# Three rounded products for each unrounded one in the causal and the cross attention of the last layer

## What is computed

```python
h = rms_norm(x, norm_g)
(qa, ka, va, ga, ub, vb, gb, qc, gc, ma, mb, mc) = split_cols(h @ w_in, IN_SPLITS)
qa, ka = partial_rope(qa, pos), partial_rope(ka, pos)          # 6 heads of 128
out_a = moba_attention(qa, ka, va) * silu(ga)                  # causal softmax(q k^T / sqrt(128)) v
out_b = gmlp_spatial_gate(ub, vb, ...) * silu(gb)
mk, mv = split(rms_norm(mem, mem_norm_g) @ w_mem_kv, 2)
out_c = softmax(qc @ mk^T / sqrt(128)) @ mv * silu(gc)         # 4 heads of 128
y = sigmoid(ma) * (out_a @ w_branch_a) + sigmoid(mb) * (out_b @ w_branch_b) + sigmoid(mc) * (out_c @ w_branch_c)
x = x + y @ w_out
```

## Time and profile before

| what | value |
|---|---|
| median of 3 runs | 913.99 us (913.52 to 914.01) |
| the profiled execution | 914.61 us |
| its span from first to last instruction | 912.4 us |
| granted TensorE clock | 1.000 |
| TensorE busy | 99% of the span |
| its weight loads busy | 84% |
| VectorE, ScalarE, GpSimd busy | 67%, 56%, 4% |
| DMA | 169.32 MB, mean 186 GB/s |

### The profile page before, as it was taken

The page is one execution under the profiler, slowest core; times in us unless marked ns, Lnnn a source line. Parts: engine busy times, 40 slices in busy tenths (PEclk is TensorE's granted clock), DMA queues, the critical chain, the costliest instruction groups (busy, mean ns, idle before and its releaser), DMA issues.

```text
span 912.4 us, 12831 instructions
## 1 busy us (share of the span) xinstructions
PE 904.5 (99%) x4764; PEld 764.8 (84%) x4764; DVE 610.7 (67%) x1007; ACT 507.8 (56%) x820; POOL 40.4 (4%) x53
## 2 busy tenths in 40 slices
PE   9999999999999999999999999999999999999997
PEld 7888788888888898878888888887888888888886
DVE  4897697766663756769766666386656577574665
ACT  5786655555562456665555555255557664655444
POOL 0100000440000001000000000001000000000000
PEclk9999999999999999999999999999999999999999
DMA  9844526777573577552855556354664465555651
GB/s 322 294 164 139 185 93 231 233 228 249 192 238 112 108 225 231 159 187 93 293 183 190 198 190 241 122 171 149 198 201 131 159 202 166 167 157 186 198 169 72
DMA packets 72604, 169.32 MB, mean 186 GB/s; under 512 B 11288, under 2 KB 32944, under 8 KB 71904
## 3 DMA queue, kind: packets, MB, share of 16 engines
q1 hardware_dynamic: 70080, 157.73, 53.3%
q0 software_dynamic: 2320, 10.58, 3.5%
q10 hardware_dynamic: 144, 0.20, 0.1%
HBM read 167.43 MB, written 1.06 MB: 185 GB/s over the span
## 4 chain that ended last, share of the span: by engine, by line
PE 95%; DVE 2%; DMA 1%; ACT 1%; SPq 0%; issue 0%; DVEq 0%; ACTq 0%
PE psum L851 20%; PE psum L1037 14%; PE psum L732 8%; PE psum L737 8%; PE psum L734 8%; PE psum L1040 8%; PE psum L1069 7%; PE psum L1073 4%; PE psum L962 3%; PE psum L972 3%; PE psum L966 3%; PE psum L1173 2%; PE psum L709 1%; PE psum L1208 1%; PE psum L1189 1%; DMA stage<-in_w_ab_in 1%
## 5 line engine op out<-in xcount | busy, mean ns | idle before, releaser
L1792 DVE TENSOR_TENSOR base_lo<-stage,base_hi 128x1024 fp32r<-128x1024 f32 (+3 forms) x221 | 261.1, 1206 | 103.9 <-ACT base_hi L1373 102.7
L1373 ACT CAST base_hi<-stage 128x1024 fp32r<-128x1024 f32 (+3 forms) x221 | 222.5, 1035 | 57.2 <-PE psum L737 22.5
L1792 DVE TENSOR_TENSOR extra_lo<-stage,extra_hi 128x1024 fp32r<-128x1024 f32 (+1 forms) x68 | 80.7, 1212 | 45.6 <-ACT extra_hi L1373 45.4
L732 PE MATMUL psum<-base_hi,xt 128*128 128x512 f32 (+2 forms) x256 | 100.7, 393 | 0.0
L737 PE MATMUL psum<-base_hi,xt 128*128 128x512 f32 (+2 forms) x256 | 98.4, 384 | 0.0
L734 PE MATMUL psum<-base_lo,xt 128*128 128x512 f32 (+2 forms) x256 | 98.2, 384 | 0.0
L1373 ACT CAST extra_hi<-stage 128x1024 fp32r<-128x1024 f32 (+1 forms) x68 | 68.1, 1029 | 46.8 <-PE psum L851 35.5
L851 PE MATMUL psum<-base_hi,ht 128*128 128x512 f32 x288 | 87.5, 393 | 0.3 <-DVE qk_t L2249 0.3
L1037 PE MATMUL psum<-xt,extra_hi 128*128 128x512 f32 x320 | 80.0, 392 | 0.0
L1037 PEld LDWEIGHTS psum<-xt,extra_hi 128*128 128x128 f32 x320 | 58.2, 189 | 10.8
L851 PEld LDWEIGHTS psum<-base_hi,ht 128*128 128x128 f32 x288 | 53.7, 188 | 12.5 <-DVE qk_t L2249 0.7
(11 more groups left out here) (265 smaller groups left out, 1538.9 us busy)
## 6 DMA issues: line engine op xcount, KB each, us to landing
stage<-in_w_up SPq DMA_DIRECT2D x80, 512.0 KB, 4.6
stage<-in_w_down SPq DMA_DIRECT2D x44, 512.0 KB, 4.4
stage<-in_w_in_a SPq DMA_DIRECT2D x22, 512.0 KB, 4.7
stage<-in_w_cd_in SPq DMA_DIRECT2D x16, 512.0 KB, 4.8
stage<-in_w_in_b SPq DMA_DIRECT2D x12, 512.0 KB, 3.6
stage<-in_w_ab_in SPq DMA_DIRECT2D x12, 480.0 KB, 6.8
ln_par<-in_ln POOLq DMA_DIRECT2D x4, 1024.0 KB, 7.6
stage<-in_w_ab_out SPq DMA_DIRECT2D x8, 512.0 KB, 3.7
```

Source lines behind the costliest of these rows:

```text
L732: pe.matmul(acc, ah, wh, start=(k == 0), stop=False)
L1373: act.copy(w_hi(c, 0, w), stage_of(c, w)).then_inc(hi_done, 1)
L1792: dve.tensor_tensor(w_lo(c, 0, w), stage_of(c, w), w_hi(c, 0, w).bitcast(F32), ALU.subtract).then_inc(lo_done, 1)
```

## The change

Every product of the ten heads becomes three of rounded operands, `hi*hi + hi*lo + lo*hi`, as in the gemms. The copies of ScalarE that already stand there write the high parts (their target gets the rounded type); VectorE makes the low parts as the difference of the source in PSUM and the high part. New are:

- `qk_low`, in VectorE's slot s, for head s: 512 columns, between the maximum and the due base_lo (causal only). TensorE's logits wait for it (`qk_lows`), and so do the transposes of the next head.
- `probs_low`, at the end of VectorE's slot s, for head s-2: 384 columns (causal) or 512 (cross). PV and the transposes of the next head's probabilities wait for it (`p_lows`).
- the high part of the causal values, 1536 columns, by ScalarE behind its slot 1, and the low part by VectorE behind its slot 2; PV waits for it (`moba_v_los`).
- the high and low parts of the cross keys, values and queries, 1024 columns each, by ScalarE at the chunks 3, 4, 5 of `gate_a` and by VectorE at 4, 5, 6; the first cross logits wait for all three (`cross_los`).

The parts lie in memory that is free by then (the hidden activations' buffer, the arena), some in the place of their source. No transfer is added.

```diff
...
@@ TensorE, slot @@
                 if stream == "moba" and h < hi_h:
                     if h >= 1:
                         pe.wait_ge(qk_copied, h)
+                        pe.wait_ge(qk_lows, h)
...
                     if h >= 1:
                         pe.wait_ge(head_done, h)
+                    pe.wait_ge(p_lows, h + 1)
+                    if stream == "moba":
+                        pe.wait_ge(moba_v_los, 1)
+                        v_hi, v_lo, p_lo, at = moba_v_hi, moba_v_lo, moba_p_lo, h * HD2
+                    else:
+                        v_hi, v_lo, p_lo, at = cross_v_hi, cross_v_lo, cross_p_lo, (h - MOBA_H) * HD2
                     for kt in range(TT):
                         first = 0 if hd.full else kt * P
-                        last = pe.matmul(psum[:, O_BANK, first:S], hd.v(kt),
-                                         probs_t[:, h % 2, kt * S:kt * S + S - first], start=(kt == 0), stop=(kt == 1))
+                        acc, cut = psum[:, O_BANK, first:S], slice(kt * S, kt * S + S - first)
+                        pe.matmul(acc, v_hi[:, kt, at:at + HD2], cross_p_hi[:, h % 2, cut], start=(kt == 0), stop=False)
+                        pe.matmul(acc, v_hi[:, kt, at:at + HD2], p_lo[:, h % 2, cut], start=False, stop=False)
+                        last = pe.matmul(acc, v_lo[:, kt, at:at + HD2], cross_p_hi[:, h % 2, cut], start=False,
+                                         stop=(kt == 1))
...
                         pe.wait_ge(p_copied, h)
+                        pe.wait_ge(p_lows, h)
...
+                    if stream == "xa":
+                        n = h - MOBA_H
+                        pe.wait_ge(cross_los, 3)
+                        for t in range(TT):
+                            acc = psum[:, LOGIT_BANK, t * S:(t + 1) * S]
+                            q_hi, q_lo = [m[:, n, t * P:(t + 1) * P] for m in (cross_q_hi, cross_q_lo)]
+                            pe.matmul(acc, q_hi, cross_k_hi[:, n, :], start=True, stop=False)
+                            pe.matmul(acc, q_hi, cross_k_lo[:, n, :], start=False, stop=False)
+                            last = pe.matmul(acc, q_lo, cross_k_hi[:, n, :], start=False, stop=True)
+                        last.then_inc(logits_ready, 1)
+                        return
+                    pe.wait_ge(qk_copied, h + 1)
+                    pe.wait_ge(qk_lows, h + 1)
+                    hi, lo = moba_qk_hi[:, h % 2, :], moba_qk_lo[:, h % 2, :]
                     for t in range(TT):
                         nk = S if t else n0
-                        last = pe.matmul(psum[:, LOGIT_BANK, t * n0:t * n0 + nk], q[:, t * P:(t + 1) * P], k[:, 0:nk],
-                                         start=True, stop=True)
+                        acc, q, k = psum[:, LOGIT_BANK, t * n0:t * n0 + nk], slice(t * P, (t + 1) * P), slice(S, S + nk)
+                        pe.matmul(acc, hi[:, q], hi[:, k], start=True, stop=False)
+                        pe.matmul(acc, hi[:, q], lo[:, k], start=False, stop=False)
+                        last = pe.matmul(acc, lo[:, q], hi[:, k], start=False, stop=True)
...
@@ ScalarE @@
-                    act.copy(qk_t[:, h % 2, :], psum[:, QK_BANK, :]).then_inc(qk_copied, 1)
+                    act.copy(moba_qk_hi[:, h % 2, :], psum[:, QK_BANK, :]).then_inc(qk_copied, 1)
...
-                    act.copy(probs_t[:, h % 2, 0:w], psum[:, PT_BANK, 0:w]).then_inc(p_copied, 1)
+                    act.copy(cross_p_hi[:, h % 2, 0:w], psum[:, PT_BANK, 0:w]).then_inc(p_copied, 1)
...
+            def moba_v_high():
+                slot("moba", 1)
+                act.copy(moba_v_hi[:, :, :], a2[:, :, 2 * AW:3 * AW]).then_inc(moba_v_his, 1)
...
+                                  3: lambda: cross_hi(cross_k_hi[:, :, :], mem_k, read("mem_k", 2)),
+                                  4: lambda: cross_hi(cross_v_hi[:, :, :], mem_v, read("mem_v", 1)),
+                                  5: lambda: cross_hi(cross_q_hi[:, :, :], q_c, read("in_c", 2)), 7: xa_first})
...
@@ VectorE, slot @@
+                def probs_low():
+                    g = lo_h + s - 2
+                    if lo_h <= g < hi_h:
+                        lows, w = (moba_p_lo, 3 * P) if stream == "moba" else (cross_p_lo, 4 * P)
+                        dve.wait_ge(p_copied, g + 1)
+                        dve.tensor_tensor(lows[:, g % 2, 0:w], psum[:, PT_BANK, 0:w],
+                                          cross_p_hi[:, g % 2, 0:w].bitcast(F32), ALU.subtract).then_inc(p_lows, 1)
+
+                def qk_low():
+                    g = lo_h + s
+                    if stream == "moba" and g < hi_h:
+                        dve.wait_ge(qk_copied, g + 1)
+                        dve.tensor_tensor(moba_qk_lo[:, g % 2, :], psum[:, QK_BANK, :],
+                                          moba_qk_hi[:, g % 2, :].bitcast(F32), ALU.subtract).then_inc(qk_lows, 1)
+
                 h = lo_h + s - 1
                 if not lo_h <= h < hi_h:
+                    qk_low()
+                    probs_low()
                     return
...
+                qk_low()
                 split_to(done["due"])
                 dve.wait_ge(exp_ready, h + 1)
...
                 last.then_inc(head_scaled, 1)
+                probs_low()
...
+            def moba_v_low():
+                slot("moba", 2)
+                dve.wait_ge(moba_v_his, 1)
+                v = a2[:, :, 2 * AW:3 * AW]
+                dve.tensor_tensor(moba_v_lo, v, moba_v_hi[:, :, :].bitcast(F32), ALU.subtract).then_inc(moba_v_los, 1)
...
+                                  4: lambda: cross_low(1, cross_k_lo[:, :, :], mem_k, cross_k_hi[:, :, :]),
+                                  5: lambda: cross_low(2, cross_v_lo[:, :, :], mem_v, cross_v_hi[:, :, :]),
+                                  6: lambda: cross_low(3, cross_q_lo[:, :, :], q_c, cross_q_hi[:, :, :]), 7: slots("xa", 1)})
...
```

More of the change, by code:

```diff
@@ L305, in build_program @@
         arena = sb("arena", [P, ARENA])
+        rounded = lambda name, at, shape: nc.alloc_sbuf_tensor_at(name, [P, *shape], F32R, offset=at)
+        cross_q_hi, cross_k_hi = [rounded(f"cross_{m}_hi", arena_at + 4 * (B2 + n * XA_H * S), [XA_H, S])
+                                  for n, m in enumerate("qk")]
+        cross_v_hi = rounded("cross_v_hi", arena_at + 4 * (B2 + 2 * XA_H * S), [TT, CW])
+        cross_p_lo = rounded("cross_p_lo", arena_at + 4 * (B2 + 3 * XA_H * S), [2, 2 * S])
+        cross_q_lo = rounded("cross_q_lo", arena_at + 4 * A2, [XA_H, S])
+        cross_k_lo = rounded("cross_k_lo", arena_at + 4 * MEM_K, [XA_H, S])
+        cross_v_lo = rounded("cross_v_lo", arena_at + 4 * MEM_V, [TT, CW])
         extra_hi = nc.alloc_sbuf_tensor_at("extra_hi", [P, NS, SLOT], F32R, offset=arena_at + 4 * EXTRA)
@@ L310, in build_program @@
         no_mask = sb("no_mask", [P, 256])
+        qk_t_at = nc.sbuf_base
         qk_t = sb("qk_t", [P, 2, 512])
+        moba_qk_hi = rounded("moba_qk_hi", qk_t_at, [2, 2 * S])
         pair_probs = sb("pair_probs", [P, 4, 384])
@@ L314, in build_program @@
         pair_st = sb("pair_st", [P, 2, 5, 4])
+        probs_t_at = nc.sbuf_base
         probs_t = sb("probs_t", [P, 2, 512])
+        cross_p_hi = rounded("cross_p_hi", probs_t_at, [2, 2 * S])
+        moba_v_lo = rounded("moba_v_lo", arena_at + 4 * A2, [TT, 3 * AW])[:, :, 2 * AW:3 * AW]
+        moba_v_hi = rounded("moba_v_hi", ht_at + 4 * 2 * S * 6, [TT, AW])
+        moba_qk_lo = rounded("moba_qk_lo", ht_at + 4 * 2 * S * 9, [2, 2 * S])
+        moba_p_lo = rounded("moba_p_lo", ht_at + 4 * 2 * S * 11, [2, 2 * S])
         ln_par = sb("ln_par", [P, 2, D])
@@ L362, in build_program @@
         p_turned, p_copied = sem("p_turned"), sem("p_copied")
+        cross_his, cross_los, p_lows = sem("cross_his"), sem("cross_los"), sem("p_lows")
+        qk_lows, moba_v_his, moba_v_los = sem("qk_lows"), sem("moba_v_his"), sem("moba_v_los")
         pv_ready, head_done = sem("pv_ready"), sem("head_done")
@@ L1712, in last_gates @@
                 slot("moba", 0)
-            gemm("in_b", columns_from(2560), {0: last_gates, **{s: slots("moba", s) for s in range(1, 10)},
+            def moba_v_high():
+                slot("moba", 1)
+                act.copy(moba_v_hi[:, :, :], a2[:, :, 2 * AW:3 * AW]).then_inc(moba_v_his, 1)
+            gemm("in_b", columns_from(2560), {0: last_gates, 1: moba_v_high,
+                                              **{s: slots("moba", s) for s in range(2, 10)},
                                               14: lambda: [deviation(4, 0, 1), deviation(4, 1, 1)]})
@@ L2309, in gmlp_norm @@
                 last.then_inc(vn_ready, 1)
-            gemm("in_b", None, {**{s: slots("moba", s) for s in range(1, 10)}, 13: gmlp_stats, 15: gmlp_norm})
+            def moba_v_low():
[3 more added lines that the diff above has]
+                dve.tensor_tensor(moba_v_lo, v, moba_v_hi[:, :, :].bitcast(F32), ALU.subtract).then_inc(moba_v_los, 1)
```

(9 more changed lines are left out.)

10 lines of the change are left out of this document (4 added, 6 removed).

## The result

The changed kernel takes 926.29 us (median of 4 executions, 924.36 to 926.68) against 914.0 before: ratio 1.0132, 95% interval 1.0117 to 1.0147. The forecast was 927.2 us, with 923 to 932 as its range. The profiled execution took 924.36 us, the fastest of the four, with a span of 922.1 us against 912.4.

What follows compares the result with a forecast made beforehand. The prediction took always-busy TensorE to bound the kernel, so its added time and new waits count: -1.9 + 3.4 (products) + 11.7 (waits) = +13.2 us, 927.8 on the profiled execution, 927.2 on the median, range 923 to 932.

Steps and rivals of the forecast that it cites:

- The waits: TensorE in both attentions idles for VectorE's late low parts: 7.5 us causal plus 4.2 cross, 11.7 us in all.
- The 0.2 us from VectorE's end to PV: Estimate added to each wait for the signal and the weight load TensorE can't start ahead: 0.2 us.
- The products: Three rounded products per unrounded one in both attentions: 1.9 us gained at 256 columns, 3.4 us lost at 128.
- the term of the narrow ones: Twelve causal products of 128 columns, each rounded one taken at 0.167 us: 3.4 us of loss, ends 1.8 and 5.1.
- The load row: Weight load on TensorE at 0.83 ns a column, 107 ns for 128 columns, would set the pace of narrow products.
- The clock: Rival: standing still in slot 3 and nine times in all drops TensorE's clock to 1.2 GHz; 930 to 933 us, chance 0.08.
- The main step: TensorE gets new idle time waiting for VectorE's subtractions in both attentions, 11.7 us, which can't be made up later.
- Edits at nothing: ScalarE's high part of V, cross casts and lows in gate_a, later base_lo, DMA queues and PSUM copies: no cost.
- Products alone: Rival: lows are made inside VectorE's free time, TensorE meets none of the waits; 915.5 us, chance 0.06.
- faster: Rival: lows hidden likewise and narrow products not paced by the load, 66 ns each; 911.9 us, chance 0.03.
- Doesn't do what it says: Rival: rounded operands run at the unrounded price everywhere; +40.7 us, 955 us, chance 0.01.

Runs made afterwards that it cites:

- the products alone: Changed kernel with three rounded products everywhere, the high part in each low part's place, no low-part subtractions or waits for them: 913.07 us, ratio 0.9987.
- the run with the wait filled: Changed kernel with ten rounded products of 512 columns issued on TensorE in slot 3 where it would wait for V's low part: 924.41 us.
- The longer wait: Changed kernel with one more pass over V (1536 columns) on VectorE ahead of its low part: 927.78 us, 926.20 to 930.59.
- the waits alone: Changed kernel with one unrounded product of the high parts in place of each three rounded ones, all casts, subtractions and waits kept: 926.62 us, ratio 1.0137.
- V's low part early: Changed kernel with both parts of the causal V made during in_ga, ahead of the attention: 922.56 us.

## Why the prediction was right, point by point

**The waits: right, nearly slot by slot.** The forecast was 7.5 us causal and 4.2 us cross; against the products alone they measure 7.5 and 4.2. The single slots, as the distance of starts in the changed kernel less that of before, are slot 2 0.3 (forecast 0.5), slot 3 2.5 (2.7), slot 4 1.0 (1.0), slot 5 1.0 (1.0), slot 6 1.4 (1.45), slot 7 0.8 (0.84), cross 1.3 each (1.4). These add up to 7.0 and 4.0. The rest is at the edges of the groups: with the products alone transposes and PV start 0.35 us apart and not 0.44 (the rows below, slot 3), and in slots 6, 7 and the cross slots the first product of PV takes 0.20 us behind a wait and 0.12 without. The sums agree better than the single slots, and that is luck in part.

```profile
695.72 0.60 PE L1105 MATMUL psum<-ident,arena 128*128 128x128 f32 x4
696.07 0.36 PE L1121 MATMUL psum<-cross_p_hi,moba_v_hi 128*128 128x256 f32 x1
```

Slot 8 had no wait, as said, and neither had the last cross PV. The terms: qk_low measures 0.60 in the queue (0.61), the causal probs_low 0.47 (0.48), V's low part 1.75 alone (1.68 in the queue). The 0.2 us from VectorE's end to PV was between the measured values: 0.30 in slot 4, 0.26 in slots 5 and 6, and 0.15 in slot 3 and the cross slots. In slot 4 the chain itself came out 0.09 shorter than the sum. The list of waits names eight waits and not nine, 9.5 us: slot 2's 0.3 us is hidden behind what still drains from the array.

**The products: the term of the narrow ones was mis-sized.** At 256 columns the starts inside a group are 0.12 us apart, as taken from the earlier trace rows. At 128 columns I took 0.167 us, the middle between the load's pace and the price of an unrounded product. They start 0.11 us apart (705.06, 705.17, 705.28 above); the first of three takes 0.07 us behind wider products (704.99 to 705.06) and 0.14 behind transposes (705.55 to 705.69). Three are 0.29 in PV and 0.37 in the logits, so 0.33, and 12 of them lose 1.4 us, not 3.4. The load row was the right neighbour: 107 ns for 128 columns by the slope of the earlier trace rows. The Trainium skill's section "LDWEIGHTS" ("TensorE: Matmul & The Clock Gate") gives the same 107, and the trace agrees. The isolated gap of 56 ns at 128 columns, from the section "Back-to-back issue gap" of the same page of the Trainium skill, is half of the 111 ns seen; that section says itself that it under-counts where each product has a weight load, and gives about 81 ns for that case, which isn't reached here either.

In sum the products save 0.8 to 0.9 us (913.07 against 913.9 and 914.0), where the forecast had them cost 1.5: even the sign was wrong. The measured terms give -1.9 + 1.4 = -0.5. The rest has the size of the edges, which the sum left out. The first product of 256 columns behind another kind takes 0.17 to 0.21 us (704.56 to 704.76), and the unrounded groups had an edge too: the first two products of the chunk behind the logits started 0.42 us apart before (702.84 and 703.26) and start 0.24 apart now (706.32 and 706.56). I haven't added these up. A slip of no weight is the old price at 128 columns: the row's 0.44 us over three distances give 0.113 us a record, not 0.107.

**The clock: a rival that came true in part.** I gave the fall of the clock a chance of 0.08. By the times it seems to happen in most executions: the medians are 925.4 and 926.3, and only two of eight lie at the 924.4 of the run with the wait filled or below; a profile of the changed kernel shows it in one of two. The mechanism was as named, its price was not. I had twelve products at twice their time, 2.8 us. With the fall the causal part took 793.97 - 684.00 = 109.97 us, without it 109.47, so 0.5 us in that profile. The longer wait says the same: 111.81 us, where the 1.8 us of longer waiting alone would make 111.3. VectorE keeps its pace while TensorE is slow, so the wait of the next slot goes (three waits for moba_p_lo and 2.7 us, against four and 3.6). What the executions at 926 us and more have beyond that no profile shows; it stays open.

**So the forecast hit as closely as it did by two errors that cancel, which is luck:** 2.4 us too much for the products, and 1 to 2 us too little for the clock. The runs give 913.07 + 11.7 = 924.8 us for the products and the waits, near the 924.4 of the run with the wait filled. The main step, 11.7 us of waits, was no luck.

**Edits at nothing: right.** The last cross low ran from 791.79 to 793.01 and the first cross logits started at 793.46, so there was 0.4 us to spare in the place where I had counted 0.2 and called it no cover. No product waited for base_lo in either attention.

**The rivals.** "Products alone" and "faster" are refuted by the waits alone, which take 926.6 us, and by the waits in the changed kernel's own list. "Doesn't do what it says" is refuted by the products alone, which take 913.1 us.

## What to carry to other kernels

When an engine that is always busy gets a new wait, the price isn't read from the other engine's busy share (VectorE was a third idle before and after). It is the length of the other engine's queue from the event that starts it to the new operation, less the time until the full engine asks. Before accepting that price, look at what stands in the queue ahead of the operation: here the same subtractions, put ahead of work that isn't due or into an earlier stage, took 11.7 to 12.6 us back. An order that is best for one kind of head needn't be for the next: where VectorE waits for a long exponential anyway, the work that isn't due belongs ahead of it.

## What the runs showed of the hardware that I had not expected

One wait of 2.4 us, in a kernel that keeps TensorE 98% busy, was enough for its granted clock to fall to the lower level in one profile of the changed kernel (0.80 and 0.77 on average in two stretches of 4 us) and not in the other. Five profiles hold a wait of 2.3 us or more in this place, and three of them show the fall: the changed kernel run again, the waits alone and the longer wait. With useless products in that gap the kernel took 924.4 us, against 925.4 and 926.3. The seven other waits, of 0.65 to 1.25 us each, left the clock at 1.00 in the first profile of the changed kernel, and so did the seven in the profile of V's low part early.

A fall costs less than the clock that it takes where another engine sets the pace just behind it. The stretches at 0.80 and 0.77 took 4 x 0.20 + 4 x 0.23 = 1.7 us of clock (an estimate from these two rows), and the causal part was 0.5 us longer.
